# A two-block inference kernel: squares, first weight slots and the fourth modulation unit rearranged in its head

## What is computed

```python
m = silu(cond) @ w_ada + b_ada                 # 6 vectors of 1024: shift, scale, gate, twice; for c and c_ctx
y = x * rsqrt(mean(x * x) + EPS) * g           # rmsnorm over the 1024 columns
h = y * (1 + scale) + shift                    # modulate
q, k, v, r = split(h @ gla_w_in)               # gla_project
z = (h @ gate_w1) @ gate_w2 + gate_b           # gate: rank 16, then 512 columns, forwards and backwards
```

## Time and profile before

| | |
|---|---|
| time, median of 3 runs | 1368.34 us (1367.38 to 1369.62) |
| the profiled execution | 1368.0 us, its span 1366.2 us |
| PE busy | 1331.7 us, 97% of the span |
| ScalarE, VectorE, GpSimd busy | 50%, 42%, 52% |
| granted clock of TensorE, mean | 0.996 of full |

### The profile page before, as it was taken

How to read it: one execution, slowest core, us unless ns; L and a number is a source line. 1 busy time by engine, 2 the same in 40 slices (tenths; PEclk the granted TensorE clock), 3 DMA queues, 4 the chain that set the end, 5 groups by cost and what they waited for, 6 DMA issues and landing times.

```text
span 1366.2 us, 22286 instructions
## 1 busy us (share of the span) xinstructions
PE 1331.7 (97%) x8270; PEld 1113.1 (81%) x8270; DVE 579.1 (42%) x1070; ACT 677.8 (50%) x1038; POOL 706.7 (52%) x307
## 2 busy tenths in 40 slices
PE   4999999999999999999999999999999999999999
PEld 0678787776888888888758746999999987999999
DVE  4414575324534443310035645455532485455510
ACT  1553134433544444432236845576675667666642
POOL 0433002243344444444344302598899775698897
PEclk9999999999999999999999999999999999999999
DMA  9423644253433333233454370566667541566564
GB/s 363 158 79 95 226 151 158 94 199 139 149 98 92 95 104 92 92 108 108 154 210 170 108 270 8 166 214 191 193 200 212 175 141 61 166 193 196 192 208 124
DMA packets 60118, 210.20 MB, mean 154 GB/s; under 512 B 6416, under 2 KB 9744, under 8 KB 59920
## 3 DMA queue, kind: packets, MB, share of 16 engines
q1 hardware_dynamic: 59616, 207.52, 46.0%
q10 hardware_dynamic: 432, 1.70, 0.3%
HBM read 208.15 MB, written 1.05 MB: 153 GB/s over the span
## 4 chain that ended last, share of the span: by engine, by line
PE 92%; DMA 3%; ACT 2%; SPq 1%; DVE 1%; issue 1%; POOL 0%; ACTq 0%
PE ps L312 72%; DMA raw<-wstream 3%; PE ps L410 2%; PE ps L933 2%; PE ps L357 1%; PE ps L927 1%; PE ps L358 1%; PE ps L919 1%; PE ps L349 1%; PE ps L1264 1%; SPq L288 1%; PE ps L1243 1%; PE ps L860 1%; PE ps L913 1%; PE ps L1224 1%
## 5 line engine op out<-in xcount | busy, mean ns | idle before, releaser
L301 POOL TENSOR_TENSOR wlo<-raw,whi 128x1024 fp32r<-128x1024 f32 x291 | 694.4, 2405 | 644.2 <-ACT whi L296 643.6
L296 ACT ACTIVATE whi<-raw 128x1024 fp32r<-128x1024 f32 x291 | 306.4, 1055 | 238.6 <-PE ps L312 143.9
L312 PE MATMUL ps<-Hhi_,whi 128*128 128x256 f32 (+1 forms) x1344 | 392.5, 320 | 0.0
L312 PE MATMUL ps<-Hlo_,whi 128*128 128x256 f32 (+1 forms) x1344 | 387.9, 316 | 0.0
L312 PEld LDWEIGHTS ps<-Hhi_,whi 128*128 128x128 f32 x1344 | 252.5, 188 | 26.7 <-issue 5.4
L312 PEld LDWEIGHTS ps<-Hlo_,whi 128*128 128x128 f32 x1344 | 252.5, 188 | 20.0 <-issue 1.9
L312 PE MATMUL ps<-Hhi_,wlo 128*128 128x256 f32 (+1 forms) x1344 | 233.6, 316 | 0.0
L312 PEld LDWEIGHTS ps<-Hhi_,wlo 128*128 128x128 f32 x1344 | 196.0, 188 | 18.4
L312 PE MATMUL ps<-hidhi,whi 128*128 128x256 f32 (+1 forms) x528 | 151.1, 315 | 0.0
L312 PE MATMUL ps<-hidlo,whi 128*128 128x256 f32 (+1 forms) x528 | 150.7, 314 | 0.0
L650 ACT ACTIVATE u<-ps,par 128x256 f32<-128x256 f32 (+1 forms) x132 | 83.8, 635 | 119.3 <-PE ps L312 110.4
(11 more groups left out here) (305 smaller groups left out, 1619.3 us busy)
## 6 DMA issues: line engine op xcount, KB each, us to landing
raw<-wstream SPq DMA_DIRECT2D x387, 512.0 KB, 3.6
XT<-x_t SPq DMA_DIRECT2D x1, 1024.0 KB, 10.7
XT<-ctx_t SPq DMA_DIRECT2D x1, 1024.0 KB, 12.1
memx<-mem_t ACTq DMA_DIRECT2D x1, 1024.0 KB, 5.5
out_t<-XT SPq DMA_DIRECT2D x1, 640.0 KB, 6.2
par<-params SPq DMA_DIRECT2D x1, 457.5 KB, 3.0
glac<-gla_consts SPq DMA_DIRECT2D x1, 384.0 KB, 9.7
out_t<-XT SPq DMA_DIRECT2D x3, 128.0 KB, 2.0
```

The source lines that it names most:

```text
L296: nc.scalar.activation(whi[:, n % RING, :], raw[:, r % RAWS, :], ACT.Copy).then_inc(S["hi_ready"], 1)
L301: nc.gpsimd.tensor_tensor(wlo[:, r, :], raw[:, r, :], whi[:, n % RING, :].bitcast(F32), ALU.subtract).then_inc(S["lo_ready"], 1)
L312: mm = nc.tensor.matmul(o, a, b, start=start, stop=stop)
```

## The change

- `half_unit` splits unit 2 in the queue: its first two slots (8, 9), then gate (10) and gq 0 (11), then its last two (12, 13), then unit 3 (14 to 17), gq 1 to 3 (18 to 20). `unit_slot` finds a slot of a unit by this.
- `TAKEN` ranks slots 12 to 17 ahead of 10 and 11.
- SyncE issues slots 8 to 17 (`LATE` = 10) ahead of `glac` and `w2`.
- The eight squares go from VectorE to ScalarE (`ACT.Square` into four places of `Hf0` in turn); VectorE makes a copy and seven sums. Later waits on `n_sq` count eight more.
- TensorE makes the norm's sum ahead of unit 2; behind unit 2 come two filler matmuls, the turn of batch 0, three more.
- ScalarE makes the hi parts of gate and gq 0 ahead of the row copy of batch 0.
- Unit 3 isn't multiplied in the head but in `first_tiles`: two slots behind k 0, two behind k 1; the turn of batch 1 is behind k 2, and its row copy on ScalarE ahead of k 3.

```diff
--- before.py
+++ after.py
@@ -28,6 +28,7 @@
 EPS = 1e-6
 RING = 4
 RAWS = 8
+LATE = 10
 FF_T = 2816 // P
 CH = 64
 NCH = TT // CH
@@ -59,11 +60,17 @@
     return (f"mod{layer}_{u}", name, MOD_UNIT * first, MOD_UNIT)
 
 
+def half_unit(layer, u, part_):
+
+    name, host, first, count = unit(layer, u)
+    return (f"{name}_{part_}", host, first + 2 * part_, 2)
+
+
 def whole(*names):
     return [(n, n, 0, c) for n, c in STREAM if n in names]
 
 
-QUEUE = [unit(0, 0), unit(0, 1), unit(0, 2), ("gate", "gate", 0, 1), ("gq", "gq", 0, 1), unit(0, 3), ("gq_", "gq", 1, 3)] + whole("gk", "gv")
+QUEUE = [unit(0, 0), unit(0, 1), half_unit(0, 2, 0), ("gate", "gate", 0, 1), ("gq", "gq", 0, 1), half_unit(0, 2, 1), unit(0, 3), ("gq_", "gq", 1, 3)] + whole("gk", "gv")
 QUEUE += [unit(0, u) for u in range(4, 12)] + whole("gr") + [("gr_b", "gr_b", 0, 2), unit(1, 0), ("gr_c", "gr_b", 2, 2), unit(1, 1)] + whole("go")
 QUEUE += [unit(1, 2)] + whole("up0") + [unit(1, 3)] + whole(*[f"up0_{_i}" for _i in range(10)])
 
@@ -89,10 +96,16 @@
 
 
 TAKEN = list(range(NSLOTS))
-for _early, _unit in (("gate", "mod0_3"), ("up0", "mod1_3"), ("cq", "mod1_7")):
+for _early, _unit, _slots in (("gate", "mod0_2_1", 2 + MOD_UNIT), ("up0", "mod1_3", MOD_UNIT), ("cq", "mod1_7", MOD_UNIT)):
     _before = range(RAW[_early], RAW[_unit])
-    for _rank, _slot in enumerate([RAW[_unit] + _s for _s in range(MOD_UNIT)] + list(_before)):
+    for _rank, _slot in enumerate([RAW[_unit] + _s for _s in range(_slots)] + list(_before)):
         TAKEN[_slot] = RAW[_early] + _rank
+
+
+def unit_slot(layer, u, s):
+
+    name = f"mod{layer}_{u}"
+    return RAW[name] + s if name in RAW else RAW[f"{name}_{s // 2}"] + s % 2
 
 
 def used(n):
@@ -356,10 +369,12 @@
                     o, r, q, c = ps[:, bank, 0:ntok], (n + s) % RING, RAW_OF[n + s] % RAWS, slice(k * P, (k + 1) * P)
                     nc.tensor.matmul(o, whi[:, r, c], xhi(k), start=k == 0, stop=False)
                     nc.tensor.matmul(o, wlo[:, q, c], xhi(k), start=False, stop=False)
-                if k == 0 and norm == "mix0":
-                    mod_turn(pe, 1)
                 if k >= 1:
                     low_part(k - 1)
+                if k < 2 and norm == "mix0":
+                    mod_products(pe, 0, 3, (2 * k, 2 * k + 1))
+                if k == 2 and norm == "mix0":
+                    mod_turn(pe, 1)
             low_part(KD - 1)
 
         def keep_running(pe, bank, count):
@@ -396,14 +411,14 @@
 
             return next(i for i, (L, a, b) in enumerate(BATCHES) if L == layer and a <= u < b)
 
-        def mod_products(pe, layer, u):
-
-            n, v, batch = RAW[f"mod{layer}_{u}"], u % 4, batch_of(layer, u)
+        def mod_products(pe, layer, u, slots=range(MOD_UNIT)):
+
+            v, batch = u % 4, batch_of(layer, u)
             first, last = u == BATCHES[batch][1], u == BATCHES[batch][2] - 1
             if first and batch in (3, 4):
                 pe.wait_ge(S["mod_out"], batch)
-            for s in range(MOD_UNIT):
-                r = n + s
+            for s in slots:
+                r = unit_slot(layer, u, s)
                 pe.wait_ge(raw_in[r % RAWS], 16 * (r // RAWS + 1))
                 for k in (2 * s, 2 * s + 1):
                     g = k % 4
@@ -414,7 +429,7 @@
         def mod_row(act, batch):
 
             layer, _, end = BATCHES[batch]
-            act.wait_ge(S["slot_used"], TAKEN[RAW[f"mod{layer}_{end - 1}"] + MOD_UNIT - 1] + 1)
+            act.wait_ge(S["slot_used"], TAKEN[unit_slot(layer, end - 1, MOD_UNIT - 1)] + 1)
             if batch >= 1:
                 act.wait_ge(S["mod_tr"], batch)
             nc.scalar.activation(modrow[:, :], ps[:, MOD_BANK[batch], :], ACT.Copy).then_inc(S["mod_row"], 1)
@@ -444,12 +459,13 @@
 
         def head_pe(pe):
             pe.wait_ge(S["cpad0"], 3)
-            for u in range(3):
-                mod_products(pe, 0, u)
+            mod_products(pe, 0, 0)
+            mod_products(pe, 0, 1)
             norm_pe(pe, "mix0", TT)
+            mod_products(pe, 0, 2)
+            keep_running(pe, 0, 2)
             mod_turn(pe, 0)
-            keep_running(pe, 0, 2)
-            mod_products(pe, 0, 3)
+            keep_running(pe, 0, 3)
 
         def rope_tables(dve):
 
@@ -481,22 +497,25 @@
             act.wait_ge(S["t_tab"], 1)
             nc.scalar.activation(tab[:, 0, :], Hf0[:, 5, 0:T], ACT.Sin)
             nc.scalar.activation(Hf0[:, 4, 0:T], Hf0[:, 4, 0:T], ACT.Sin).then_inc(S["t_sin"], 1)
+            act.wait_ge(S["xin"], 32)
+            for m in range(KD):
+                if m >= 4:
+                    act.wait_ge(S["n_tot"], m - 3)
+                nc.scalar.activation(Hf0[:, m % 4, :], XT[:, m, :], ACT.Square).then_inc(S["n_sq"], 1)
             norm_root(act, "mix0", TT)
-            mod_row(act, 0)
             hi_slot(act, 0)
             hi_slot(act, 1)
+            mod_row(act, 0)
 
         def head_dve(dve):
             rope_tables(dve)
-            dve.wait_ge(S["xin"], 32)
             for m in range(KD):
-                x, square = XT[:, m, :], Hf0[:, m % 2, :]
+                dve.wait_ge(S["n_sq"], m + 1)
                 if m == 0:
-                    nc.vector.tensor_tensor(rstd[:, :], x, x, ALU.mult).then_inc(S["n_tot"], 1)
-                    continue
-                dlink(nc.vector.tensor_tensor(square, x, x, ALU.mult))
-                dve.wait_ge(S["n_tot"], m)
-                nc.vector.tensor_tensor(rstd[:, :], rstd[:, :], square, ALU.add).then_inc(S["n_tot"], 1)
+                    nc.vector.tensor_copy(rstd[:, :], Hf0[:, 0, :]).then_inc(S["n_tot"], 1)
+                else:
+                    dve.wait_ge(S["n_tot"], m)
+                    nc.vector.tensor_tensor(rstd[:, :], rstd[:, :], Hf0[:, m % 4, :], ALU.add).then_inc(S["n_tot"], 1)
             mod_bias(dve, 0)
             gain_scale(dve, 0, 0, 1, 0, 8)
 
@@ -533,7 +552,7 @@
 
             N, banks = SUMMED.index(t), NBANKS[t][0]
             part_, total = ps[:, banks[m % len(banks)], 0:ntok], rstd[:, 0:ntok]
-            dve.wait_ge(S["n_sq"], KD * (N - 1) + m + 1)
+            dve.wait_ge(S["n_sq"], KD * N + m + 1)
             if m == 0:
                 ins = nc.vector.tensor_copy(total, part_)
             else:
@@ -550,7 +569,7 @@
             if t != "mix0":
                 norm_root(act, t, ntok)
             for k in range(KD):
-                if t == "mix0" and k == 2:
+                if t == "mix0" and k == 3:
                     mod_row(act, 1)
                 act.wait_ge(S["n_xn"], KD * N + k + 1)
                 for h in range(ntok // T):
@@ -2079,9 +2098,11 @@
             sp.dma_start(XT[:, :, 0:T], ctx_in).then_inc(S["xin"], 16)
             for n in range(RING, RAWS):
                 load_slot(sp, n)
+            for n in range(RAWS, RAWS + LATE):
+                load_slot(sp, n)
             sp.dma_start(glac[:, :], gla_c).then_inc(S["glac"], 16)
             sp.dma_start(w2[:, :], w2_in).then_inc(S["glac"], 16)
-            for n0, n1 in stretches(RAWS, END_SLOT, SRC):
+            for n0, n1 in stretches(RAWS + LATE, END_SLOT, SRC):
                 loops = max(0, (n1 - n0 - RAWS) // RAWS)
                 n2 = n1 - RAWS * loops
                 for n in range(n0, n2):
```

## The result

| | before | after |
|---|---|---|
| median of 7 runs | 1368.49 us (1367.38 to 1372.28) | 1376.49 us (1374.61 to 1377.10) |
| ratio, 95% interval | | 1.0051 (1.0036 to 1.0065) |
| profiled execution, span | 1366.2 us | 1374.8 us |

The changed kernel is slower by 8.0 us between the medians, by 4.9 to 8.9 us by the interval. The forecast was 1374.4, with a range to 1377.0.

The account below looks back on a forecast made before the run. Prediction: PE's unbroken run of weight products bounds the kernel, so head shifts count one for one. First products -1.5, stall +5.9, clock +1.7 sum to +6.1 us on the 1368.3 median: 1374.4, range 1371.0 to 1377.0.

Parts of the forecast that it names:

- Mechanism and sign: Behind the first products: z1 waits behind hi copies of slots 18 and 19, loaded late; slower overall, chance 0.87.
- rival 1: Behind the stall: the clock stays high or falls late, so +4.4 us, 1372.7; chance 0.20.
- rival 3: At k 4: VectorE isn't held, gain 4.5 in place of 1.5 us, total +3.1, 1371.4; chance 0.12.
- rival 4: Behind the first products: slots 18 and 19 are there in time, no stall, 1366.8 or 1363.8; chance 0.04.
- rival 5: At the norm: squares on ScalarE bring it no earlier, stall remains; chance 0.14 shared with the low-clock first-products case.
- The stall: Behind the first products: z1 copied 5.87 us later behind their end than before; bounds 5.0 to 6.4.
- Landings, squares and root: In the head: unit 2's last slot at 30.46, sums done about 23.8, root about 27.6 and not 34.3 us.
- Gain ahead of k 4: Head to first products: norm starts 4.5 us earlier, 3.0 given back at k 4, first products end 1.5 earlier.
- rival 2: In the first products: the clock is low there too, so +8.3 us, 1376.6; chance 0.14, shared with the squares case.
- The clock behind the stall: Behind PE's idle stretch, 51.3 to 57.9: work at the low clock costs 1.7 us, bounds 0 and 2.0.
- What unit 3 takes back at k 4: In the first products: ScalarE and VectorE sit behind unit 3, giving back 3.0 of the 4.5 us gained.
- The rule on the shared ports: Before the first norm: VectorE and GpSimd share ports; gain scale takes 0.17 us without POOL's low part, 2.04 beside it.

Follow-up runs that it names:

- old_queue: Changed kernel with gate and gq 0 back behind unit 2 and batch 0's row copy ahead of the hi copies: 0.9998 of the kernel before's time.
- queue_only: Kernel before with only the new slot order, gate and gq 0 between the halves of unit 2: 1.0090 of the kernel before's time.
- fill_unit2: Changed kernel plus 5 filler matmuls between unit 2's second and third slot: 1.0045 of the kernel before's time.
- fill_stall: Changed kernel plus 13 filler matmuls behind the first products, where TensorE idles: 1.0046 of the kernel before's time.
- unit3_head: Changed kernel with unit 3 back ahead of the first products, its turn behind k 0's hi products: 1.0040 of the kernel before's time.
- old_queue_unit3_head: Changed kernel with the queue of before and unit 3 ahead of the first products: 0.9964 of the kernel before's time, 0.9971 repeated.
- unit3_head_fill_stall: Changed kernel with unit 3 ahead of the first products and 13 filler matmuls behind them: 1.0002 of the kernel before's time.
- z1_first: Changed kernel with the hi copies of splits 2 and 3 moved behind the z1 copy in ScalarE's queue: 1.0022 of the kernel before's time.

## Why the prediction was right, and where it wasn't

- **Mechanism and sign: right, shown by old_queue and queue_only.** Slots 18 and 19 are held by gate and gq 0, and z1 stands behind their hi copies. Rivals 1, 3, 4 and 5 fall: the clock was low, k 4 was held, slot 18 wasn't issued before 53.05, and the squares did bring the root forward.
- **The stall, 5.87 forecast, 5.73 measured** (53.05 to 58.78). The parts, forecast and measured: 3.54 and 3.50 for the landing, 1.28 and 1.27 for the second slot, 1.05 and 0.96 for the hi copy up to the start of z1. The row taken from the kernel before carried over; the estimate from the Trainium skill, DMA: Bandwidth & Descriptors, "Anatomy of one DMA — SWDGE (gpsimd) path" (3.2 for one slot), would have been 0.3 short.
- **Landings, squares and root: right.** The last slot of unit 2 was used at 30.31 (30.46 forecast), the sums ended at 23.87 (23.8), the root at 27.64 (27.6).
- **Gain ahead of k 4: the step that failed, -1.5 forecast, +0.2 measured.** The order of the terms held: unit 3 does hold VectorE at k 4, and from the first product to the end of the turn it took 7.14 (6.95 forecast). But the start was 35.14 and not 33.75. I had PE at work since 24, at the high clock; it was idle for 2.78 us between slots 9 and 12, the clock fell at 29.8, the last slot's products took 1.92 and not 1.05, and the two fillers, which I had put under the row copy, took until 33.81, 0.9 past it. That is rival 2, but only ahead of the first products; unit 3 itself ran at the high clock. Without the fall, in fill_unit2, the 1.3 are back.
- **The clock behind the stall: 1.7 forecast, 3.7 measured, outside its bounds of 0 to 2.0.** I took the 3.9 us that the low clock lasted into new work after the first idle time for the most it could last. Here it lasted 7.9 us (59.50 to 67.4). fill_stall prices it.
- **The sum:** +0.2 + 5.7 + 3.7 = 9.6 at the second z product, +6.1 forecast. The time, +8.0 between medians, was within the range only because that reached to rival 2, and by some luck: the two errors go the same way, and the head's +9.65 alone would be 1378.1, outside it.
- **What unit 3 takes back at k 4**, 3.0 in the forecast, is 3.4 by unit3_head.
- **The rule on the shared ports** (the Trainium skill, SBUF — State Buffer, "SBUF: two separate sides") is borne out: the gain scale took 0.17 where POOL had finished and 1.93 where it hadn't (old_queue_unit3_head). In between it took 0.47, 0.37 and 0.25 (fill_stall, unit3_head_fill_stall, fill_unit2), each time ending within 0.03 us of POOL's low parts.

## What to carry to other kernels

In a ring, a slot that is loaded early but used late holds the place of the slot one turn behind it: when weights are moved forward in a load order, count which loads then wait for their use, and what stands behind those loads in each engine's queue. Moving work off a bound engine pays only up to the next thing that ends late; here splitting the change and keeping the squares, the earlier norm's sum and the late small transfers, but neither the slot order nor unit 3's new place, made the faster kernel. And the stall of TensorE had a second price behind it here, in the work that ran at the low clock; it came out larger (3.7 us) than the one read from a single earlier idle time (1.7).

## What the runs showed of the hardware that I had not expected

**The low clock's length varies for the same stall.** After an idle time of 6.3 to 6.6 us behind the first products the clock was low for 10.2 us in the profiled executions of the changed kernel (both) and of unit3_head, and for 6.8 in those of queue_only and fill_unit2; in z1_first, with 2.85 us of idling, it was 3.4. In the longest of these stretches (57.1 to 67.4) TensorE was at work without a gap from 59.50 on. What sets the length no run here shows.

**TensorE has two paces at a granted clock of 1.00.** Windows of the same stage (the second feed-forward) in the kernel before, in the changed kernel and in unit3_head:

```profile
900.00:940.00 40.00, 40.00 (x355) 40.00 (x354) 20.39 (x45) 27.25 (x45) 35.67 (x15) 1.00 0.60 190
```
```profile
900.00:940.00 40.00, 40.00 (x355) 40.00 (x354) 20.90 (x45) 28.15 (x47) 36.65 (x16) 1.00 0.63 197
```
```profile
900.00:940.00 40.00, 40.00 (x342) 40.00 (x341) 19.56 (x43) 26.04 (x42) 35.28 (x16) 1.00 0.61 184
```

355 matmuls in 40 us against 342, both with PE busy throughout, no wait and a clock of 1.00: 4% slower, for some 130 us, and then the old pace again. One matmul of 128x256 takes 276 ns in the first case and 281 in the other, so the count isn't a matter of missing records. It came in the profiled executions of unit3_head, fill_stall, queue_only and fill_unit2 at this stage (an estimate from the 4% and the 130 us is 5 us each), and in the repeat of the changed kernel, z1_first and queue_only in the third feed-forward (342 in the 40 us from 1240). All six have a second z product 4.9 us or more later than before; of the seven such executions only the first one of the changed kernel is without it, and none of the six others, the kernel before among them, has it. So it may hang on the change and not on chance; that isn't shown, and one trace of each kernel can't say how often it comes. It would fit the spread of the times, and may be why the time of unit3_head doesn't show its 4 us. What sets it I don't know; no run here tells.
